# Opening stage of a float32 layer stack: weight units loaded before x, x turned between units, GpSimd's low halves in eight pieces

## The reference, cut to what matters

```python
h = rmsnorm(x, g_pre_mix)
z = h @ w_in                              # queries, keys, values, gates of all branches
y_nsa = ...                               # compressed, selected and window attention
y_ml = mlstm_chunkwise(...)               # conv of width 4, silu, gates
kv = rmsnorm(mem, g_mem) @ w_mem_kv       # memory branch: 256 memory tokens
y_mem = softmax(q_mem @ k.T) @ v
y = gm0 * (y_nsa @ w_proj_nsa) + gm1 * (y_ml @ w_proj_ml) + gm2 * (y_mem @ w_proj_mem)
x = x + rmsnorm(y @ w_out, g_post_mix)
x = x + rmsnorm((silu(gate) * up) @ w_ffn_down, g_post_ffn)
...                                       # second block, in its second layer:
a, gate = split(h @ w_pw1 + b_pw1)
h = a * sigmoid(gate)
h = depthwise_conv(h, w_dw) + b_dw        # width 31
h = silu(layernorm(h)) @ w_pw2 + b_pw2
```

## Time and profile before

| | |
|---|---|
| median of 3 runs | 3122.21 us (3120.79 to 3123.86) |
| profiled execution, its own time | 3124.37 us |
| its span (first to last instruction) | 3122.5 us |
| PE busy | 2900.4 us, 93% |
| PEld busy | 2375.3 us, 76% |
| DVE busy | 1494.5 us, 48% |
| ACT busy | 886.2 us, 28% |
| POOL busy | 340.9 us, 11%, 70 instructions |
| granted TensorE clock, mean | 0.963 |

### The profile page before, as it was taken

The page is one execution under the profiler, slowest core; times in us unless marked ns, Lnnn a source line. Parts: engine busy times, 40 slices in busy tenths (PEclk is TensorE's granted clock), DMA queues, the critical chain, the costliest instruction groups (busy, mean ns, idle before and its releaser), DMA issues.

```text
span 3122.5 us, 34634 instructions
## 1 busy us (share of the span) xinstructions
PE 2900.4 (93%) x13386; PEld 2375.3 (76%) x13386; DVE 1494.5 (48%) x2168; ACT 886.2 (28%) x1206; POOL 340.9 (11%) x70
## 2 busy tenths in 40 slices
PE   6998799999989999899996799999999889899997
PEld 6777688888767888778885588887888765578886
DVE  2334344444456553465434744434453379555532
ACT  4333443344233222222221322222221232422211
POOL 4222111112300000000001000000000056100000
PEclk9998899999999999999998899999999999999999
DMA  6222112222342223222222123232222221122232
GB/s 194 81 65 68 54 44 78 71 71 69 120 155 68 94 94 98 91 81 94 95 97 77 59 90 106 88 101 86 99 98 90 86 68 41 62 74 94 94 98 71
DMA packets 255085, 270.43 MB, mean 87 GB/s; under 512 B 5695, under 2 KB 243407, under 8 KB 254858
## 3 DMA queue, kind: packets, MB, share of 16 engines
q1 hardware_dynamic: 250688, 261.77, 26.1%
q10 hardware_dynamic: 4298, 7.36, 0.6%
HBM read 258.62 MB, written 10.49 MB: 86 GB/s over the span
## 4 chain that ended last, share of the span: by engine, by line
PE 69%; issue 16%; DVE 6%; POOL 5%; ACT 2%; DMA 1%; SPq 0%; POOLq 0%; DVEq 0%; ACTq 0%
PE bank L1114 20%; PE bank L1115 20%; PE bank L1116 20%; POOL w_lo L1074 3%; POOL w_lo L1068 3%; PE bank L1566 1%; PE bank L1129 1%; PE bank L1131 1%; PE bank L1130 1%; DVE rstd L1989 1%; ACT w_hi L662 1%; PE bank L1142 1%; PE bank L1144 0%; PE bank L1143 0%; DVE w_lo L1954 0%
## 5 line engine op out<-in xcount | busy, mean ns | idle before, releaser
L1114 PE MATMUL bank<-h_hi,w_hi 128*128 128x512 f32 x2064 | 818.8, 397 | 54.3 <-POOL w_lo L1074 25.9
L1115 PE MATMUL bank<-h_lo,w_hi 128*128 128x512 f32 x2064 | 812.9, 394 | 0.0
L1116 PE MATMUL bank<-h_hi,w_lo 128*128 128x512 f32 x2064 | 811.7, 393 | 0.0
L1954 DVE TENSOR_TENSOR w_lo<-w_raw,w_hi 128x2048 fp32r<-128x2048 f32 (+2 forms) x176 | 390.2, 2220 | 391.7 <-ACT w_hi L662 325.7
L1114 PEld LDWEIGHTS bank<-h_hi,w_hi 128*128 128x128 f32 x2064 | 393.2, 191 | 145.3 <-POOL w_lo L1074 30.1
L1116 PEld LDWEIGHTS bank<-h_hi,w_lo 128*128 128x128 f32 x2064 | 393.1, 190 | 83.0
L1115 PEld LDWEIGHTS bank<-h_lo,w_hi 128*128 128x128 f32 x2064 | 393.2, 190 | 82.2 <-issue 1.2
L1114 PE MATMUL bank<-hid_hi,w_hi 128*128 128x512 f32 x880 | 343.9, 391 | 0.0
L1116 PE MATMUL bank<-hid_hi,w_lo 128*128 128x512 f32 x880 | 342.8, 390 | 0.0
L1115 PE MATMUL bank<-hid_lo,w_hi 128*128 128x512 f32 x880 | 342.7, 389 | 0.0
L654 ACT ACTIVATE w_hi<-w_raw 128x2048 fp32r<-128x2048 f32 x124 | 236.8, 1910 | 357.7 <-PE bank L1116 350.3
(11 more groups left out here) (355 smaller groups left out, 3448.2 us busy)
## 6 DMA issues: line engine op xcount, KB each, us to landing
w_raw<-in_ffn_w_in_dram SPq DMA_DIRECT2D x88, 1024.0 KB, 5.1
w_raw<-in_w_in_dram SPq DMA_DIRECT2D x32, 1024.0 KB, 5.3
w_raw<-in_ffn_w_out_dram SPq DMA_DIRECT2D x32, 1024.0 KB, 5.2
w_raw<-in_w_ffn_in_dram SPq DMA_DIRECT2D x22, 1024.0 KB, 5.1
w_raw<-in_ffn_w_out_dram SPq DMA_DIRECT2D x16, 768.0 KB, 4.5
w_raw<-in_conv_w_pw_dram SPq DMA_DIRECT2D x12, 1024.0 KB, 5.6
w_raw<-in_w_ffn_down_dram SPq DMA_DIRECT2D x8, 1024.0 KB, 5.1
gate_scratch<-gate_stage ACTq DMA_DIRECT2D x24, 256.0 KB, 2.0
```

The source lines that it names most:

```text
L1114: nc.tensor.matmul(bank[b][:, 0:n], wh, xh, start=first, stop=False)
L1115: nc.tensor.matmul(bank[b][:, 0:n], wh, xl, start=False, stop=False)
L1116: ins = nc.tensor.matmul(bank[b][:, 0:n], wl, xh, start=False, stop=last)
L1954: v.tensor_tensor(w_lo[slot][:, 0:n], raw[s][:, 0:n], w_hi[slot][:, 0:n].bitcast(F32), ALU.subtract).then_inc(w_lo_ready, 1)
```

## The change

Three things are changed. SP loads the first two weight units ahead of x. In all engines the work on x leaves the fixed start: ScalarE splits unit 1 before it squares x, and x is turned in two halves (`x_turn`), after unit 1 and after unit 2 in `SCHEDULE`, into banks 4 to 7; unit 0 starts when the first groups of mem are split; a root of a constant is taken on ScalarE while mem is loaded. And GpSimd's `low` and `low_in_loop` make each `w_lo` by eight instructions of 256 columns in place of one of 2048, with the semaphore's increment on the last.

```diff
-SCHEDULE = [("unit", u) for u in range(6)]
+SCHEDULE = [("unit", 0), ("unit", 1), ("x_turn", 0), ("unit", 2), ("x_turn", 1), ("unit", 3), ("unit", 4), ("unit", 5)]
...
-            for t in range(TT):
-                sp.dma_start(x_tok[:, t, :], x_rows[:, t, :]).then_inc(x_in_place, 16)
             for u, (w, c, n, kind) in enumerate(UNITS):
                 load(u // 2, u % 2, src_fixed[w][:, :, c:c + n], KT, n)
+                if u == 1:
+                    for t in range(TT):
+                        sp.dma_start(x_tok[:, t, :], x_rows[:, t, :]).then_inc(x_in_place, 16)
                 if u == 4:
 
                     sp.wait_ge(tok_turned, 16)
...
             act.wait_ge(stat_set, 1)
+            nc.scalar.activation(stat[:, 2:3], eps, ACT.Sqrt)
+
+            def sum_of_squares(src, t):
+                chain.link(act, nc.scalar.activation(junk[:, :], src, ACT.Square, accum_out=ss[:, t:t + 1]))
+
             act.wait_ge(mem_in_place, 16 * MT)
...
+            for t in range(MT):
+                sum_of_squares(mem_tok[:, t, :], t)
+            nc.scalar.activation(rs_tok[:, 0:MT], ss[:, 0:MT], ACT.Sqrt, bias=eps, scale=1.0 / D).then_inc(tok_root, 1)
             high(0)
             act.wait_ge(vec_ready, 1)
...
+            for n in range(KT):
                 act.wait_ge(tok_turned, n + 1)
...
+                nc.scalar.activation(m_hi[:, n, :], bank[n][:, 0:MEM], ACT.Copy, scale=col("g_mem", n)).then_inc(start_hi, 1)
+            high(1)
+            act.wait_ge(x_in_place, 16 * TT)
+            for t in range(TT):
+                sum_of_squares(x_tok[:, t, :], MT + t)
+            nc.scalar.activation(rs_tok[:, MT:6], ss[:, MT:6], ACT.Sqrt, bias=eps, scale=1.0 / D).then_inc(tok_root, 1)
+
+            def x_turn(half):
+                for j in range(4 * half, 4 * half + 4):
+                    act.wait_ge(tok_turned, KT + j + 1)
+                    nc.scalar.activation(h_hi[:, j, :], bank[4 + j % 4][:, :], ACT.Copy, scale=col("g_pre_mix", j)).then_inc(start_hi, 1)
...
+            def low_by_tiles(d, s, n):
+
+                for c in range(0, n, UC):
+                    part = slice(c, c + UC)
+                    ins = nc.gpsimd.tensor_tensor(w_lo[d][:, part], raw[s][:, part], w_hi[d][:, part].bitcast(F32), ALU.subtract)
+                ins.then_inc(w_lo_ready, 1)
+
             def low_in_loop(u, s):
 
                 pool.wait_ge(w_hi_ready, u + 1)
-                nc.gpsimd.tensor_tensor(w_lo[s][:, :], raw[s][:, :], w_hi[s][:, :].bitcast(F32), ALU.subtract).then_inc(w_lo_ready, 1)
+                low_by_tiles(s, s, UNIT)
 
             def low(u):
 
-                d = SLOT[u]
                 pool.wait_ge(w_hi_ready, u + 1)
-                nc.gpsimd.tensor_tensor(w_lo[d][:, :], raw[u % 2][:, :], w_hi[d][:, :].bitcast(F32), ALU.subtract).then_inc(w_lo_ready, 1)
+                low_by_tiles(SLOT[u], u % 2, UNIT)
...
+            def x_turn(half):
+                pe.wait_ge(tok_scaled, 6)
+                for j in range(4 * half, 4 * half + 4):
+                    pe.wait_ge(start_lo, 8 if half == 0 else KT + j - 3)
+                    for t in range(TT):
+                        ins = nc.tensor.transpose(bank[4 + j % 4][:, t * P:(t + 1) * P], x_tok[:, t, j * P:(j + 1) * P], ident)
+                    ins.then_inc(tok_turned, 1)
...
                 if u < 2:
-
-                    pe.wait_ge(start_lo, 12)
+                    pe.wait_ge(start_lo, 2 + 6 * u)
```

More of the change, by code:

```diff
@@ L1171, in _ @@
             ins.then_inc(vec_turned, 1)
-            for n in range(16):
+            pe.wait_ge(tok_scaled, MT)
+            for n in range(KT):
                 if n == 7:
                     pe.wait_ge(vec_ready, 1)
-                if n >= 8:
-                    pe.wait_ge(start_lo, n - 7)
-                pe.wait_ge(tok_scaled, MT if n < 8 else 6)
-                j = n % 8
-                for t in range(MT if n < 8 else TT):
-                    src = mem_tok if n < 8 else x_tok
-                    ins = nc.tensor.transpose(bank[j][:, t * P:(t + 1) * P], src[:, t, j * P:(j + 1) * P], ident)
-                ins.then_inc(tok_turned, 1)
+                for t in range(MT):
+                    ins = nc.tensor.transpose(bank[n][:, t * P:(t + 1) * P], mem_tok[:, t, n * P:(n + 1) * P], ident)
+                ins.then_inc(tok_turned, 1)
+            def x_turn(half):
[5 more added lines that the diff above has]
+                    ins.then_inc(tok_turned, 1)
             def unit(u):
@@ L1196, in unit @@
                 if kind == "mem_k":
-                    products(s, KT, n, (m_hi, m_lo), (b0, b0 + 1), MEM)
+                    products(s, KT, n, (m_hi, m_lo), (b0, b0 + 1), MEM, ready=(lambda k: pe.wait_ge(start_lo, k + 1)) if u == 0 else None)
                 elif kind == "mem_v":
@@ L1310, in ml_turn @@
                     ins.then_inc(m_turned, 1)
-            steps = {"unit": unit, "mem_scores": mem_scores, "mem_turn": mem_turn, "mem_out": mem_out, "cmp_hidden": cmp_hidden,
+            steps = {"unit": unit, "x_turn": x_turn, "mem_scores": mem_scores, "mem_turn": mem_turn, "mem_out": mem_out, "cmp_hidden": cmp_hidden,
                      "cmp_out": cmp_out, "gate_turn": gate_turn, "ml_cols": ml_cols, "ml_scores": ml_scores, "ml_out": ml_out,
@@ L1635, in _ @@
-            for n in range(16):
-                dve.wait_ge(start_hi, n + 1)
-                j = n % 8
-                if n < 8:
-                    ins = v.scalar_tensor_tensor(m_lo[:, j, :], bank[j][:, 0:MEM], col("g_mem", j), m_hi[:, j, :].bitcast(F32),
-                                                 ALU.mult, ALU.subtract)
-                else:
-                    ins = v.scalar_tensor_tensor(h_lo[:, j, :], bank[j][:, :], col("g_pre_mix", j), h_hi[:, j, :].bitcast(F32),
-                                                 ALU.mult, ALU.subtract)
-                ins.then_inc(start_lo, 1)
+            for t in range(MT):
+                v.tensor_scalar(mem_tok[:, t, :], mem_tok[:, t, :], rs_tok[:, t:t + 1], None, ALU.mult).then_inc(tok_scaled, 1)
@@ new lines, in _ @@
+            for n in range(KT):
+                dve.wait_ge(start_hi, n + 1)
+                v.scalar_tensor_tensor(m_lo[:, n, :], bank[n][:, 0:MEM], col("g_mem", n), m_hi[:, n, :].bitcast(F32),
+                                       ALU.mult, ALU.subtract).then_inc(start_lo, 1)
+            dve.wait_ge(tok_root, 2)
+            link(v.reciprocal(rs_tok[:, MT:6], rs_tok[:, MT:6]))
+            for t in range(TT):
+                v.tensor_scalar(x_tok[:, t, :], x_tok[:, t, :], rs_tok[:, MT + t:MT + t + 1], None, ALU.mult).then_inc(tok_scaled, 1)
@@ L1646, in unit, with x_turn @@
+            def x_turn(half):
+                for j in range(4 * half, 4 * half + 4):
+                    dve.wait_ge(start_hi, KT + j + 1)
+                    v.scalar_tensor_tensor(h_lo[:, j, :], bank[4 + j % 4][:, :], col("g_pre_mix", j), h_hi[:, j, :].bitcast(F32),
+                                           ALU.mult, ALU.subtract).then_inc(start_lo, 1)
             def unit(u):
@@ L1804, in ml_turn @@
                     mark(v.tensor_tensor(yml[1][:, h, :], bank[h][:, :], yml[0][:, h, :].bitcast(F32), ALU.subtract), m_lo_s, h + 1)
-            steps = {"unit": unit, "mem_scores": mem_scores, "mem_turn": mem_turn, "mem_out": mem_out, "cmp_place": cmp_place,
+            steps = {"unit": unit, "x_turn": x_turn, "mem_scores": mem_scores, "mem_turn": mem_turn, "mem_out": mem_out, "cmp_place": cmp_place,
                      "cmp_out": cmp_out, "ml_rows": ml_rows, "ml_cols": ml_cols, "ml_scores": ml_scores, "ml_out": ml_out,
```

29 lines of the change are left out of this document (4 added, 25 removed).

## The result

The changed kernel takes **3127.98 us** (median of 9 runs, 3126.42 to 3135.17) against 3122.21 (9 runs, 3120.52 to 3123.86) for the kernel before beside it: ratio 1.0024, 95% interval 1.0014 to 1.0034. It is slower, by 7.5 us by the ratio. I had said 3168, and 3130 at the least. The direction was right, the size was not: I had forecast a loss of 46.5 us.

A forecast was written before the change was run, and what follows sets the result against it. TensorE, busy 93% of the span, was taken to lose time only where it waits, notably for w_lo. Terms -3 + 0.5 - 2 + 3.5 + 47 + 0.5 = +46.5 us gave 3168 us, range 3130 to 3186.

The forecast's parts named there:

- opening: Start of the kernel: unit 0 starts 13 us sooner, about 3 arrive at unit 5; -3 us (0 to -8).
- 180 to 250 us: One w_lo wait grows, +0.5 us; VectorE's gate_row instruction gets in after a piece, -2 us (+2 to -4).
- merge: Near 820 us: VectorE instructions slip between pieces, so TensorE waits longer for w_lo; +3.5 us (+1 to +7).
- convolution: Between 2500 and 2665 us: pieces starve in two VectorE chains and TensorE waits; +47 us, first unit after it +0.5.
- step 1: Convolution, low half of b1: two pieces run, six starve until the first chain ends; ready at 2557.2.
- step 4: Convolution, low half of b3: five pieces starve through a later chain; pair 3 starts 46.8 us late.
- first to ask gets it: Rival, chance 0.05: a waiting piece goes before VectorE's next chain instruction; +15 us over three pairs, 3135.
- price of the eight pieces: Each w_lo on GpSimd: eight pieces in a row take 5.1 us, +0.5 us over one instruction.

The follow-up runs named there:

- e1: The changed kernel with its new opening, but every w_lo one instruction of 2048 columns again; 3115.23 us, ratio 0.9979 to the kernel before.
- e12: e1 with 256-column pieces for the w_lo of units 0 to 5 alone; 3112.81 us, ratio 0.9982 to the kernel before.
- e13: e1 with 256-column pieces for the w_lo of the fixed units from 6 on, up to about 420 us; 3117.09 us, ratio 0.9993.
- e5: e1 with 256-column pieces for the w_lo of the convolution; 3124.74 us, ratio 1.0012 to the kernel before.
- e6: e1 with four pieces of 512 columns for each w_lo of the convolution; 3113.57 us, ratio 0.9978 to the kernel before.
- e7: e1 with two pieces of 1024 columns for each w_lo of the convolution; 3113.55 us, ratio 0.9976 to the kernel before.
- e2: The kernel before, its opening untouched, with every w_lo in 256-column pieces; 3133.88 us, ratio 1.0041.
- e3: The changed kernel, but the convolution's eleven w_lo each one instruction of 2048 columns again; 3121.60 us, ratio 1.0002 to the kernel before.
- e8: e1 with cmp_w1's four loads moved behind unit 5's load on SP's queue; 3108.17 us, ratio 0.9960 to the kernel before.
- e14: The kernel before with cmp_w1's four loads moved behind unit 5's load, nothing else; 3118.02 us, ratio 0.9990.

## Why the prediction was wrong

| term | predicted | measured |
|---|---|---|
| opening | -3 (0 to -8) | -6.6 (e1), +1 for its pieces (e12) |
| 180 to 250 us | -1.5 | +4.4 (e13 less e1) |
| merge | +3.5 | 0.5 or less (trace) |
| convolution | +47.5 | +10 (four traces; e5 less e1: +10.3) |

**The step that failed is step 1 of the convolution**: "one more piece, then the chain starts", and "six pieces starve until it ends", and step 4 with it. I took "GpSimd thus got nothing done while the chain ran" for a property of the chain. It is one of the moment of asking. Those two `w_lo` were asked for beside the twelfth and sixteenth unbroken instruction. In the changed kernel the pieces of low b1 stand there already when the chain starts, break it every 1.14 us, and VectorE never reaches eight. The next question, at 2527.80, comes beside the sixth, since eight pieces in the chain take until 2524.31 where one instruction was over at 2519.15 in e1. So the pieces do change who starves, but through how long they keep breaking the chain, not through their size. The sizes between fit: in e6 the four pieces of low b1 are over 6.1 us after the first was asked for, and the next question comes beside the tenth unbroken instruction; in e7 they take 4.9 us and it comes beside the eleventh. Both starve.

**The rivals.** What came is the one that I called "first to ask gets it" and gave 0.05: 0.5 us for each piece (I had 0.6), "+15 over three pairs", 3135. I dismissed it by the starved `w_lo`, and both are true, each on its side of the eighth instruction. By the rule of the Trainium skill (SBUF — State Buffer, Who interferes with whom), whichever issues first holds the port and the other blocks; the runs agree up to the seventh unbroken VectorE instruction and not beyond. Over the three pairs it came to 6.9 us and not 15. The chains grew by 11.0, 7.6 and 3.9 us, 22.5 in all; chain 2 sees only one `w_lo` (33.10 us, have 29.24 for the chain ahead of it). From conv_h to the start of its chain each pair is shorter, by 12.1 us together: the holds of 4.90 and 4.78 us are gone, as I had said, and a third ahead of chain 2, which I had left out. And two waits of VectorE for TensorE's taps, 3.4 us, are gone as well. The rest of the 10 us is the 2.6 ahead of pair 0, where I had 0.5, and what lies behind pair 3.

**The opening's term was too small.** The start of unit 0 and of cmp_w1's loads came out within 0.2 us. Mis-sized was what of it arrives at unit 5. Its load was issued at 46.71 in place of 51.70, 5.0 us earlier where I had 2.1, since SP was through with cmp_w1's four loads in 4.8 us and not 7.8. Its weights took 10.5 us to land in place of 12.2, and its `w_lo` 1.0 us longer: 5.6 us at unit 5's start in this trace. At its end it is 8.4, because the kernel before ran the first 6.1 us of it at a granted clock of 0.5 of full speed (1.2 GHz), behind its wait, and the changed one did not. Kernels with the same opening scatter mostly by this: e1, e6, e7 and e5 have the same instructions up to 2490 us and lead the trace of before there by 6.6, 8.2, 12.1 and 14.4 us, and up to 2480 us their traces have 188, 184, 180 and 175 us at the lower level. So one trace against one is good to some 4 us, and only the timed runs settle a few.

**180 to 250 us had the wrong sign.** VectorE's gate_row instruction did get in after a piece (1.17 us in place of 5.03), and a wait of TensorE of 5.3 us that followed it is gone. But the first `w_lo` there grew from 4.6 to 8.18 us and TensorE waits 3.77 us for it; with both, the changed kernel gains 1.0 us on e1 between 214 and 255 us. Then TensorE waits 4.75 us for the `w_lo` at 252.88 (7.11 us long), where e1 has no wait and which I had not looked at, and that is more than the gain. Between 215 and 420 us the traces with pieces there lose 2.4 (changed), 1.2 (e2), 2.0 (e3) and 3.0 us (e13) of their lead over the kernel before, and e1 loses 0.1. So the sign is shown; the 4.4 us of the timed runs are more than any trace has, and the size stays between 1 and 5 us.

**Merge.** The `w_lo` there grew as I had said: four of the six from 796 us on take 7.1 to 7.6 us, where one took 4.6, with VectorE instructions between their pieces.

```profile
796.45 7.60 POOL L1075 TENSOR_TENSOR w_lo<-w_raw,w_hi 128x256 fp32r<-128x256 f32 x8 [5.22 <-ACT w_hi L655]
```

What I undersized is what VectorE's earlier end gives back. Its holds of 4 to 5 us in the merge are gone, and it is done with the second pass at 827.2 us in place of 836.8. TensorE's waits for `w_lo` are two of 9.1 us in all (the longest 4.8) in place of three of 10.5 (6.0). Between 800 and 900 us the changed kernel loses 0.3 us of its lead and e1, with whole `w_lo`, 0.8: no cost shows.

The price of the eight pieces, +0.5, was +1.0 when undisturbed, inside the bounds that I gave. The measured terms of the table, the merge taken as nothing, add up to +9.1 us where the changed kernel lost 7.5. With an interval of about 3 us on each that is agreement.

## What to carry to other kernels

Before cutting an instruction that shares a port with a long chain, ask beside which instruction of the chain it is asked for. Here one asked for late in the chain waited to its end and took most of its time where VectorE had no use for the port, which was the better of the two, since VectorE set the pace; cut into pieces it took 4 us out of VectorE each time. What the change gained was loads put in the order in which they are needed; the same question asked of the queue behind (cmp_w1's loads ahead of unit 5's) was worth about as much again (6 us by the ratios of e8 and e1, 3 in e14), and with whole `w_lo` it makes 3108.
